# First block's mixer, front part: pooling as shifted sums with its counts in the weights, one rotation product per query head, gate half before value half, gate bias as one product

## The chip, the cores and the metric

The kernel runs on one core of one Trainium2 chip. The metric is the device time of one execution in microseconds (us), of which the median over runs counts. Engines are TensorE (PE, with PEld for its weight loads), VectorE (DVE), ScalarE (ACT), GpSimd (POOL) and SyncE (SP, which issues most DMAs).

## What is computed

The program is a chain of two transformer models over a sequence of 512 tokens of width 1024. The change touches only the mixer of the first model, which has two layers (`b0` and `b1`). Cut to what matters:

```python
p = h @ w_in[l]                       # 384 q, 256 kv, 32 k_rope, 256 pooling, 256 u, 256 v
# attention: latent queries and keys, 8 heads, 64 columns without and 32 with rotation
cq, ckv = rmsnorm(h_q, q_norm), rmsnorm(h_kv, kv_norm)
q_rope = [t1 * cos - t2 * sin, t1 * sin + t2 * cos]
s = q_nope . k_nope + q_rope . k_rope ; p = softmax(s * scale) ; out = p @ v
# pooling: groups of 64 columns, windows 2, 4, 8, 16 centred on t and clipped to the sequence
mean = (cs[hi] - cs[lo]) / (hi - lo)
out_g = (mean - h_g) @ w_pool[g] * pool_scale
# spatial gate: u and v, 4 heads of 64 columns, chunks of 128 tokens
z = gelu(h_uv) ; u, v = split(z) ; v = rmsnorm(v per head)
mixed = einsum('gpq,bcqgd->bcpgd', w_s, v) + b_s
out = u * mixed
```

After it come the output projection and the feed-forward of each layer, then the second model.

## The kernel before, in words

All activations are held with features on partitions and the 512 tokens along the free dimension. Every engine has its own program, written out by hand, and waits on semaphores (`wait_ge(..., at(engine, mark))`) for a mark that another engine sets when its instruction is done (`did(engine, mark)`). There is no scheduler: an engine works strictly in the order of its program, so whatever stands behind a waiting instruction waits too.

Large products take float32 numbers as a high and a low part (`hH`, `hL`; weights `WH`, `WL`) and add three products per 128 rows (`three`, L2621). Weights come in numbered chunks through two slots: SP loads `raw` (`load`, L503), ScalarE rounds it to `WH` (`hi`, L757), GpSimd subtracts to get `WL` (`low_parts`, L698), TensorE waits for that (`chunk`) and marks the slot as used. `c` is the first chunk of the layer's `w_in`; `c + 4` and `c + 5` hold u and v.

`first_mixing(l)` exists once for each engine. TensorE's goes: projections q, kv, k_rope and pooling (`p0`, `p1`) into the four banks `G`; sums of squares for the two norms; `spread_roots` (L2754), which spreads a norm's reciprocal roots over all partitions and waits for VectorE's reciprocal (L1494); u into `S[0]`, `S[1]`; v token by token chunk into `G[k]` (256 columns); the transposes of `w_s` (L2915); eight query heads through four banks `G[h % 4]`; the pooling products (L2941); 16 gate products (L2949), each followed by one that adds the bias (L2950, one partition row against `ones`); keys and values; then the attention loop, whose first instruction is the score product L2975.

VectorE's goes: rotation of the key (`rotate`, L1799 to L1802: two products and a sum); the norm of q (L1517 and L1509 in turn with ScalarE's rounding L814); clearing the padded rows `prow` and `pw` and copying `p0`, `p1` (L1629 to L1634); the norm of kv; for both halves of the pooling columns all four window sizes as shifted sums (L1649), each wanted half multiplied by the reciprocal counts `pool_inv` (L1656) and less the row itself (L1659); the statistics of v (L1666 to L1672); the rotation of each query head, three instructions with a 32 x 512 shape; the scaling of v (L1682, L1685); the pooled and gated outputs parted into high and low (L1527, L1529); eight copies of the rotated key (L1703); the attention loop.

The wait that ties them: a query head's product into a bank waits until VectorE has rotated the head that was in it.

```python
if h >= 4:
    pe.wait_ge(dve_done, at("dve", f"{n}.q{h - 4}.r"))
...
rotated_queries(0, 2)
V.tensor_tensor(v3, v3, vr[:, :].unsqueeze(2).broadcast_to([P, 16, 64]), ALU.mult)
```

## Time and profile before

| what | value |
|---|---|
| three runs, median | 3288.6 us (3285.46 to 3291.47) |
| the profiled execution, its own time | 3287.65 us |
| its span (first to last instruction) | 3285.8 us |
| mean granted TensorE clock over the span | 0.977 |
| TensorE busy | 3156.8 us, 96% |
| VectorE busy | 1878.1 us, 57% |
| front part of the mixer in layer 0, from the first u product to the first score product | 73.33 to 162.23 us |

The page gives shares of the whole span. The front part touched here is some 89 us long and comes twice, so it is read by stretches and in order of time. A granted clock of 1.0 is 2.4 GHz, 0.5 is 1.2 GHz. A float32 product that is not split into high and low parts shows as two records (xcount 2 for one instruction). The span is 1.85 us shorter than the execution's own time.

### The profile page before, as it was taken

Reading aid. Unit: us, or ns where it says so; the run is one execution under the profiler, and the core shown is the slowest. Engines: PE = TensorE matmul, PEld = TensorE weight load, DVE = VectorE, ACT = ScalarE, POOL = GpSimd, SP = SyncE. Lnnn points to the kernel's source line nnn. Section 1 sums busy time; section 2 is a strip of 40 time slices with the busy share of each in tenths; the row PEclk is TensorE's granted clock in tenths of the full one; section 3 lists DMA queues with packets and bytes.
Section 4 is the critical chain, followed back from the end, with each engine's and each line's share of the span. In section 5 each row is a group of like instructions: output and inputs, shape, how many; then the busy total and the mean of one; then the engine's idle time right before and its main releaser. Section 6 shows DMA issues by size and latency. Waiting matters only on the chain.

```text
span 3285.8 us, 42019 instructions
## 1 busy us (share of the span) xinstructions
PE 3156.8 (96%) x16648; PEld 2576.4 (78%) x16648; DVE 1878.1 (57%) x2970; ACT 1173.5 (36%) x1843; POOL 1245.3 (38%) x562
## 2 busy tenths in 40 slices
PE   8899999998999999999999999889999999999998
PEld 7647888876479888777888998758888687778887
DVE  4764777847544554674435877559665538453223
ACT  4353222232545433323336555332222325432222
POOL 4203444533037433334245454224444320134443
PEclk9899999998999999999999999899999999999999
DMA  7203545523035322223233333225554220113331
GB/s 131 61 13 95 157 142 174 181 66 71 13 95 165 99 87 81 77 71 96 90 110 104 111 111 112 98 70 179 160 178 137 77 73 14 39 58 97 97 96 64
DMA packets 480370, 324.40 MB, mean 99 GB/s; under 512 B 102336, under 2 KB 447552, under 8 KB 479664
## 3 DMA queue, kind: packets, MB, share of 16 engines
q1 hardware_dynamic: 475472, 310.10, 32.2%
q10 hardware_dynamic: 2656, 6.30, 0.5%
q0 software_dynamic: 2048, 5.32, 0.5%
q8 instruction: 132, 2.16, 0.3%
q14 instruction: 62, 0.51, 0.0%
HBM read 316.41 MB, written 5.24 MB: 98 GB/s over the span
## 4 chain that ended last, share of the span: by engine, by line
PE 85%; DVE 10%; ACT 3%; POOL 1%; issue 1%; DMA 0%; DVEq 0%; ACTq 0%; POOLq 0%
PE G L2630 11%; PE G L2631 11%; PE G L2635 11%; PE G L2621 11%; PE G L2846 6%; PE G L2847 5%; PE G L2851 5%; PE G L2646 2%; PE S L2975 2%; PE M L3052 2%; PE G L3693 1%; POOL WL L698 1%; PE S L2621 1%; ACT WH L757 1%; PE G L3042 1%
## 5 line engine op out<-in xcount | busy, mean ns | idle before, releaser
L698 POOL TENSOR_TENSOR WL<-raw,WH 128x1024 fp32r<-128x1024 f32 (+1 forms) x520 | 1224.6, 2377 | 1920.5 <-ACT WH L757 1920.5
L757 ACT ACTIVATE WH<-raw 128x1024 fp32r<-128x1024 f32 (+1 forms) x520 | 492.3, 995 | 607.4 <-PE G L2851 425.4
L2630 PE MATMUL G<-hH,WH 128*128 128x512 f32 x1520 | 594.8, 391 | 0.0
L2631 PE MATMUL G<-hL,WH 128*128 128x512 f32 x1520 | 591.9, 389 | 0.0
L2635 PE MATMUL G<-hH,WL 128*128 128x512 f32 x1520 | 360.1, 389 | 0.0
L2630 PEld LDWEIGHTS G<-hH,WH 128*128 128x128 f32 x1520 | 285.4, 188 | 60.7 <-ACT t_s L1198 0.8
L2635 PEld LDWEIGHTS G<-hH,WL 128*128 128x128 f32 x1520 | 285.3, 188 | 59.3
L2631 PEld LDWEIGHTS G<-hL,WH 128*128 128x128 f32 x1520 | 285.4, 188 | 58.7
L1550 DVE SCALAR_TENSOR_TENSOR acc<-adaw,cvec,acc 128x512 f32<-128x512 f32 x280 | 250.7, 948 | 4.2
L2621 PE MATMUL G<-hH,WH 128*128 128x512 f32 (+1 forms) x400 | 155.7, 389 | 14.8 <-POOL WL L698 14.8
L2621 PE MATMUL G<-hH,WL 128*128 128x512 f32 (+1 forms) x400 | 152.9, 382 | 0.0
L2621 PE MATMUL G<-hL,WH 128*128 128x512 f32 (+1 forms) x400 | 152.9, 382 | 0.0
L1574 DVE TENSOR_TENSOR FH<-silu,G 128x512 fp32r<-128x512 f32 x44 | 30.3, 688 | 212.7 <-PE G L2635 156.6
L2846 PE MATMUL G<-FH,WH 128*128 128x512 f32 x352 | 143.0, 406 | 0.2 <-DVE xT L1590 0.2
L2847 PE MATMUL G<-FL,WH 128*128 128x512 f32 x352 | 140.7, 400 | 0.0
L824 ACT ACTIVATE silu<-G 128x512 f32<-128x512 f32 x44 | 26.3, 599 | 271.5 <-PE G L2635 262.8
L1577 DVE TENSOR_TENSOR FL<-silu,FH 128x512 fp32r<-128x512 f32 x44 | 107.5, 2444 | 1.5
L1487 DVE TENSOR_TENSOR rstd<-rstd,sq 128x512 f32<-128x512 f32 (+1 forms) x84 | 61.5, 732 | 78.9 <-ACT sq L795 73.3
L1574 DVE TENSOR_TENSOR m_FH<-m_silu,G 128x512 fp32r<-128x512 f32 x22 | 15.1, 688 | 149.8 <-PE G L2635 147.5
L2621 PEld LDWEIGHTS G<-hH,WH 128*128 128x128 f32 x400 | 77.1, 193 | 30.0 <-POOL WL L698 15.7
L2621 PEld LDWEIGHTS G<-hL,WH 128*128 128x128 f32 x400 | 77.0, 192 | 14.5 <-issue 0.7
L2621 PEld LDWEIGHTS G<-hH,WL 128*128 128x128 f32 x400 | 76.9, 192 | 14.4
(699 smaller groups left out, 6402.7 us busy)
## 6 DMA issues: line engine op xcount, KB each, us to landing
raw<-ffn_w_in_in SPq DMA_DIRECT2D x264, 256.0 KB, 3.4
adaw<-ada_w_in SPq DMA_DIRECT2D x48, 1024.0 KB, 5.3
raw<-ab_w_in_in SPq DMA_DIRECT2D x128, 256.0 KB, 3.0
raw<-ffn_w_out_in SPq DMA_DIRECT2D x96, 256.0 KB, 2.9
raw<-w_gate_in SPq DMA_DIRECT2D x88, 256.0 KB, 3.3
raw<-w_up_in SPq DMA_DIRECT2D x88, 256.0 KB, 3.4
raw<-w_down_in SPq DMA_DIRECT2D x64, 256.0 KB, 2.9
raw<-w_in_in SPq DMA_DIRECT2D x40, 256.0 KB, 3.3
```

The costliest lines, as they stand in the source:

```text
L698: nc.gpsimd.tensor_tensor(WL[c % 2][:, cut], raw[c % 2][:, cut], WH[c % 2][:, cut].bitcast(F32), ALU.subtract)\
L757: nc.scalar.activation(WH[c % 2][:, cut], raw[c % 2][:, cut], ACT.Copy).then_inc(weights_hi, 1)
L1550: V.scalar_tensor_tensor(sums[:, b, i, :], weights[h % 2][:, k, :], col, sums[:, b, i, :], ALU.mult, ALU.add)\
L1577: V.tensor_tensor(FL[:, j, :], silu[:, t % 2, :], FH[:, j, :].bitcast(F32), ALU.subtract).then_inc(dve_done, did("dve", f"{n}.FL{t}"))
L2621: last = mm(dst, x, y, start=(k == 0 and j == 0), stop=(k == K - 1 and j == 2))
L2630: mm(dst, view(WH[c % 2], k), high, start=(k == 0 and not (joint and i)), stop=False)
L2631: mm(dst, view(WH[c % 2], k), low, start=False, stop=False)
L2635: last = mm(dst, view(WL[c % 2], k), X(k)[0], start=False, stop=(k == K - 1 and not (joint and i == 0)))
L2646: last = mm(dst, x, y, start=(k == 0 and j == 0 and not (joint and i)), stop=(k == K - 1 and j == 2 and not (joint and i == 0)))
L2846: mm(dst, part(WH, k, cols, o), high, start=(k == 0 and not (joint and i)), stop=False)
L2847: mm(dst, part(WH, k, cols, o), low, start=False, stop=False)
L2851: last = mm(dst, part(WL, k, cols, o), X(k)[0], start=False, stop=(k == count - 1 and not (joint and i == 0)))
```

## The change

- Pooling. ScalarE, no longer VectorE, copies `p0` and `p1` to `prow`. Only the window sizes that a half needs are summed; the last goes straight to `pd`. There is no product with counts: 1/w is multiplied into `w_p` once per layer, the first and last 8 tokens are corrected by `edges`, and the subtraction of the row is a second TensorE product with `w_n = -w_p`. Window work of half 0 stands before the q norm, of half 1 inside it.
- Order on TensorE. v (the gate half) comes in chunk `c + 4`, before u in `c + 5`; the spread of the kv norm stands between v1 and v2; then pooling products, transposes of `w_s`, u into `G[0]`, `G[1]`; query heads 0 to 3; the gate products; query heads 4 to 7; keys and values.
- Gate bias. One 33-row product of 512 columns per half opens the bank (L2982 of the changed kernel), in place of 16 products.
- Rotation. `qT` and `kT` use all 128 rows: 32 rows q times cos and 32 rows swapped q times sin, against the rotated key in both. The score product adds them, so a head takes one VectorE instruction.
- GpSimd's start gets four small clears and one DMA more; SP's table shrinks from 1024 to 34 columns.

The diff, cut to its core:

```diff
-    cols["pool_inv"] = inv.reshape(P, -1)
...
+        edge[r, g // 2] = np.stack([w / inside[:8], w / inside[T - 8:]])
+        share[r, g // 2] = 1.0 / w
+    cols["pool_edge"] = np.concatenate([share, edge.reshape(P, -1)], axis=1)
...
-                for n in range(3):
...
+                for n, block in enumerate((0, 2, 1)):
...
+                    load(c + 3 + n, columns(c + 3 + n, w, r0 + ROPE + block * 2 * P))
...
+                    nc.gpsimd.memset(b_s[:, :, :], 0.0).then_inc(pool_done, 1)
+                    nc.gpsimd.memset(bsel[:, :], 0.0).then_inc(pool_done, 1)
+                    pool.wait_ge(pool_done, 5)
+                    for g in range(2):
+                        nc.gpsimd.memset(bsel[32 * g:32 * g + 1, 64 * g:64 * g + 64], 1.0).then_inc(pool_done, 1)
...
+                    pool.dma_start(b_s[32 * g:32 * g + 1, :, :], a["b_s"][l:l + 1].rearrange("o (k g) p -> o g k p", g=2)[:, g]).then_inc(sides_loaded, 16)
...
-                stats(f"{n}.nq", 3, lambda k: latq[:, k, :], lat_fresh)
...
+                def pool_rows(k):
+                    act.wait_ge(pe_done, at("pe", f"{n}.p{k}"))
+                    nc.scalar.activation(prow[:, k, PAD:PAD + T], G[2 + k][:, :], ACT.Copy).then_inc(act_done, did("act", f"{n}.prow{k}"))
+
+                def gate_rows(k):
+                    act.wait_ge(pe_done, at("pe", f"{n}.v{k}"))
+                    nc.scalar.activation(vg[:, k, :], G[k][:, 0:SGW], ACT.Gelu_apprx_tanh).then_inc(act_done, did("act", f"{n}.vg{k}"))
+
+                for k in range(3):
+                    if k == 2:
+                        pool_rows(0)
+                    square(f"{n}.nq", k, latq[:, k, :], lat_fresh)
+                stats_before[0] = f"{n}.nq.sum"
+                root(f"{n}.nq", T // P, QL)
                 for k in range(2):
...
+                pool_rows(1)
...
+                gate_rows(0)
+                gate_rows(1)
...
+                gate_rows(2)
+                gate_rows(3)
+                hi(c + 6)
+                act.wait_ge(dve_done, at("dve", f"{n}.vrec"))
+                nc.scalar.activation(vr[:, :], vr[:, :], ACT.Sqrt).then_inc(act_done, did("act", f"{n}.vr"))
+                act.wait_ge(pe_done, at("pe", f"{n}.wsT"))
+                nc.scalar.activation(w_sT[:, :, :].rearrange("p g q -> p (g q)"), G[2][:, :], ACT.Copy).then_inc(act_done, did("act", f"{n}.wsT"))
...
+                    nc.scalar.activation(ug[:, k, :], G[k][:, :], ACT.Gelu_apprx_tanh).then_inc(act_done, did("act", f"{n}.ug{k}"))
...
+                V.tensor_scalar(w_n[:, :, :], w_p[:, :, :], -1.0, None, ALU.mult).then_inc(dve_done, did("dve", f"{n}.wn"))
...
+                    V.tensor_scalar(w_p[:, k, :], w_p[:, k, :], pool_edge[:, k:k + 1], None, ALU.mult).then_inc(dve_done, did("dve", f"{n}.wp"))
+                for o in (PAD - 8, PAD + T):
+                    V.memset(prow[:, :, o:o + 8], 0.0).then_inc(dve_done, did("dve", f"{n}.pz"))
...
-                rotate(n, "kr", G[1], krope[64:96, :])
...
-                V.memset(prow[:, :, :], 0.0).then_inc(dve_done, did("dve", f"{n}.pz"))
-                V.memset(pw[:, :, :], 0.0).then_inc(dve_done, did("dve", f"{n}.wz"))
...
-                    V.tensor_copy(prow[:, k, PAD:PAD + T], G[2 + k][:, :]).then_inc(dve_done, did("dve", f"{n}.prow{k}"))
...
+                V.tensor_copy(krope[96:128, :], krope[64:96, :]).then_inc(dve_done, did("dve", f"{n}.kr.2"))
...
+                def windows(k):
+
+                    dve.wait_ge(act_done, at("act", f"{n}.prow{k}"))
+                    src = prow[:, k, :]
+                    for w, (back, ahead) in enumerate(((1, 0), (1, -1), (2, -2), (4, -4))[:2 * k + 2]):
+                        dve.wait_ge(dve_done, here())
+                        if w % 2 and w // 2 == k:
+                            V.tensor_tensor(pd[64:128, k, :], src[64:128, PAD - back:PAD - back + T], src[64:128, PAD - ahead:PAD - ahead + T], ALU.add)\
+                                .then_inc(dve_done, did("dve", f"{n}.w{k}{w}"))
+                            continue
...
                         V.tensor_tensor(dst[:, o:o + m], src[:, o - back:o - back + m], src[:, o - ahead:o - ahead + m], ALU.add)\
                             .then_inc(dve_done, did("dve", f"{n}.w{k}{w}"))
...
-                            V.tensor_tensor(pd[r:r + 64, k, :], dst[r:r + 64, PAD:PAD + T], pool_inv[r:r + 64, k, :], ALU.mult)\
-                                .then_inc(dve_done, did("dve", f"{n}.pm{k}{w}"))
...
-                            V.tensor_tensor(pd[r:r + 64, k, :], pd[r:r + 64, k, :], prow[r:r + 64, k, PAD:PAD + T], ALU.subtract)\
...
+                            V.tensor_copy(pd[0:64, k, :], dst[0:64, PAD:PAD + T]).then_inc(dve_done, did("dve", f"{n}.pc{k}"))
+                    dve.wait_ge(dve_done, here())
+                    for e, o in enumerate((0, T - 8)):
+                        V.tensor_tensor(pd[:, k, o:o + 8], pd[:, k, o:o + 8], edges[:, k, e, :], ALU.mult).then_inc(dve_done, did("dve", f"{n}.pd{k}"))
+
+                windows(0)
+                mean(f"{n}.nq")
+                windows(1)
+                normed(f"{n}.nq", 3, lambda k: latq[:, k, :], lambda k: g_q[:, l, k:k + 1], cqH, cqL)
+                mean(f"{n}.nkv")
+                normed(f"{n}.nkv", 2, lambda k: latkv[:, k, :], lambda k: g_kv[:, l, k:k + 1], ckH, ckL)
...
+                def rotated_query(h):
+
+                    dve.wait_ge(pe_done, at("pe", f"{n}.qh{h}"))
+                    V.tensor_tensor(qT[64:128, h, :], G[(h + 3) % 4][64:128, :], trig[64:128, :], ALU.mult).then_inc(dve_done, did("dve", f"{n}.q{h}.r"))
...
-                        rotate(n, f"q{h}", G[h % 4], qT[64:96, h, :])
...
+                    V.tensor_scalar(hH[:, 4 + k, :], S[k][:, :], g_pool[:, l, k:k + 1], None, ALU.mult).then_inc(dve_done, did("dve", f"{n}.mH{4 + k}"))
...
+                    V.scalar_tensor_tensor(hL[:, 4 + k, :], S[k][:, :], g_pool[:, l, k:k + 1], hH[:, 4 + k, :].bitcast(F32), ALU.mult, ALU.subtract)\
...
+                for h in range(4):
+                    rotated_query(h)
+                    if h in (1, 2):
+                        pooled(h - 1)
+                for h in range(4, NH):
+                    rotated_query(h)
+                    if h % 2:
+                        k = h // 2 - 2
+                        dve.wait_ge(pe_done, at("pe", f"{n}.sg{k}"))
+                        dve.wait_ge(act_done, at("act", f"{n}.ug{k}"))
+                        dve.wait_ge(dve_done, here())
+                        V.tensor_tensor(ht[:, k, :], M[k][:, :], ug[:, k, :], ALU.mult).then_inc(dve_done, did("dve", f"{n}.sgo{k}"))
+                        parted(6 + k, n)
...
-                    V.tensor_copy(kT[64:96, h, :], krope[64:96, :]).then_inc(dve_done, did("dve", f"{n}.kr{h}"))
...
+                    V.tensor_copy(kT[64:128, h, :], krope[64:128, :]).then_inc(dve_done, did("dve", f"{n}.kr{h}"))
...
-                project(c + 4, 0, S[0], "u0")
-                project(c + 4, 1, S[1], "u1")
...
-                spread_roots(f"{n}.nkv")
...
+                        spread_roots(f"{n}.nkv")
+                        pe.wait_ge(act_done, at("act", f"{n}.prow1"))
...
+                    pe.wait_ge(dve_done, at("dve", f"{n}.pd{k}"))
+                    mm(S[k][:, :], w_p[:, k, :], pd[:, k, :], start=True, stop=False)
+                    mm(S[k][:, :], w_n[:, k, :], prow[:, k, PAD:PAD + T], start=False, stop=True).then_inc(pe_done, did("pe", f"{n}.pool{k}"))
+                pe.wait_ge(sides_loaded, 16 * SIDES * (l + 1))
+                pe.wait_ge(act_done, at("act", f"{n}.vg2"))
+                for g in range(4):
+                    last = nc.tensor.transpose(G[2][:, g * P:g * P + P], w_s[:, g, :], ident[:, :])
+                last.then_inc(pe_done, did("pe", f"{n}.wsT"))
+                chunk(c + 5)
+                project(c + 5, 0, G[0], "u0")
+                project(c + 5, 1, G[1], "u1")
                 tally.also("pe", f"used.{c + 5}")
...
+                        if h < 4:
+                            pe.wait_ge(act_done, at("act", f"{n}.{('vg3', 'ug0', 'ug1', 'wsT')[h]}"))
+                        else:
+                            pe.wait_ge(act_done, at("act", f"{n}.qn{h - 4}"))
+                            pe.wait_ge(dve_done, at("dve", f"{n}.q{h - 4}.r"))
...
+                queries(0, 4)
...
-                    mm(S[k][:, :], w_p[:, k, :], pd[:, k, :], start=True, stop=True).then_inc(pe_done, did("pe", f"{n}.pool{k}"))
...
+                    mm(M[k][:, :].rearrange("p (c t) -> p c t", c=4), bsel[:, :], b_s[:, k, :].unsqueeze(1).broadcast_to([33, 4, P]), start=True, stop=False)
...
-                            mm(dst, vg[:, c4, head * 64:head * 64 + 64], w_sT[:, head, :], start=True, stop=False)
-                            last = mm(dst, ones[0:1, 0:64], b_s[0:1, head * P:head * P + P], start=False, stop=True)
...
+                            last = mm(dst, vg[:, c4, head * 64:head * 64 + 64], w_sT[:, head, :], start=False, stop=(c4 == 3))
...
+                queries(4, NH)
...
-                        mm(S[s % 2][:, :], qT[0:QK, h, i * P:i * P + P], kT[0:QK, h, :], start=True, stop=True).then_inc(pe_done, did("pe", f"{n}.sc{s}"))
...
+                        if i == 0:
+                            pe.wait_ge(dve_done, at("dve", f"{n}.kr{h}"))
+                        mm(S[s % 2][:, :], qT[:, h, i * P:i * P + P], kT[:, h, :], start=True, stop=True).then_inc(pe_done, did("pe", f"{n}.sc{s}"))```

**VectorE, layer 0, behind the key's rotation.** `ncol` is the reciprocal of a norm, `ht` the normed row. Before:

```order
L1494 RECIPROCAL ncol<-M 128x4
L1517 SCALAR_TENSOR_TENSOR ht<-latq,g_q,M 128x512 x2
L1509 TENSOR_TENSOR cqL<-ht,cqH 128x512
L1517 SCALAR_TENSOR_TENSOR ht<-latq,g_q,M 128x512
L1509 TENSOR_TENSOR cqL<-ht,cqH 128x512 x2
L1629 MEMSET prow 128x1088
L1630 MEMSET pw 128x1088
L1634 COPY prow<-G 128x512 x2
L1494 RECIPROCAL ncol<-M 128x4
```

Of the change:

```order
L1522 RECIPROCAL ncol<-M 128x4
L1681 TENSOR_TENSOR pw<-prow 128x526
L1681 TENSOR_TENSOR pw<-pw 128x524
L1681 TENSOR_TENSOR pw<-pw 128x520
L1686 COPY pd<-pw 64x512
L1675 TENSOR_TENSOR pd<-pw 64x512
L1689 TENSOR_TENSOR pd<-pd,pool_edge 128x8 x2
L1545 SCALAR_TENSOR_TENSOR ht<-latq,g_q,M 128x512 x2
L1537 TENSOR_TENSOR cqL<-ht,cqH 128x512
L1545 SCALAR_TENSOR_TENSOR ht<-latq,g_q,M 128x512
L1537 TENSOR_TENSOR cqL<-ht,cqH 128x512 x2
L1522 RECIPROCAL ncol<-M 128x4
```

The clears and copies behind the q norm are gone, and the sums of half 1 now stand between the q norm's reciprocal and its first row. The second reciprocal still comes last.

**TensorE, layer 0, end of the v products.** `WH_54`, `WH_55` are the two weight slots. Before (the end of v1, the transposes, the start of v2):

```order
L2621 MATMUL G<-WL_57,hH 128x256
L2621 MATMUL G<-WH_55,hL 128x256
L2915 MATMUL S<-ident,w_s 128x128 x4
L2621 MATMUL G<-WH_55,hH 128x256
L2621 MATMUL G<-WL_57,hH 128x256
```

Of the change (the end of v3, then the start of u):

```order
L2654 MATMUL G<-WL_56,hH 128x256
L2654 MATMUL G<-WH_54,hL 128x256
L2947 MATMUL S<-pd,w_p 128x512
L2948 MATMUL S<-prow,w_n 128x512
L2947 MATMUL S<-pd,w_p 128x512
L2948 MATMUL S<-prow,w_n 128x512
L2952 MATMUL G<-ident,w_s 128x128 x4
L2654 MATMUL G<-hH,WH_55 128x512
L2654 MATMUL G<-hL,WH_55 128x512
```

The pooling products moved from behind the queries to here, doubled, and u follows v.

**TensorE, layer 0, the gate products.** Before, behind query head 7 (the last two rows come eight times for each half):

```order
L2621 MATMUL G<-cqL,WH_55 128x512
L2621 MATMUL G<-cqH,WL_57 128x512
L2941 MATMUL S<-pd,w_p 128x512 x2
L2949 MATMUL M<-w_sT,vg 64x128
L2950 MATMUL M<-b_s,ones 64x128
```

Of the change, between query heads 3 and 4:

```order
L2654 MATMUL G<-cqH,WL_56 128x512
L2982 MATMUL M<-b_s,bsel 128x512
L2987 MATMUL M<-w_sT,vg 64x128 x8
L2982 MATMUL M<-b_s,bsel 128x512
L2987 MATMUL M<-w_sT,vg 64x128 x8
L2654 MATMUL G<-cqH,WH_55 128x512
```

Sixteen bias products became two, and the stretch has query heads on both sides.

## Rows read from the trace of the kernel before

**Rows 1.** The page: busy time by engine; the chain that ended last.
```profile
PE 3156.8 (96%) x16648; PEld 2576.4 (78%) x16648; DVE 1878.1 (57%) x2970; ACT 1173.5 (36%) x1843; POOL 1245.3 (38%) x562
PE 85%; DVE 10%; ACT 3%; POOL 1%; issue 1%; DMA 0%; DVEq 0%; ACTq 0%; POOLq 0%
```

**Rows 2.** TensorE in order of time, block 0 (start us, us, engine, line ...).
```profile
73.33 0.48 PE L2621 MATMUL S<-hH,WH 128*128 128x512 f32 x1
...
84.31 1.05 PE L2754 MATMUL M<-ident,ncol 128*128 128x128 f32 x8
85.12 0.36 PE L2621 MATMUL G<-WH,hH 128*128 128x256 f32 x1
...
90.96 0.60 PE L2915 MATMUL S<-ident,w_s 128*128 128x128 f32 x4
...
97.87 0.47 PE L2621 MATMUL G<-cqH,WH 128*128 128x512 f32 x1 [0.56 <-ACT vg L887]
...
106.10 0.40 PE L2621 MATMUL G<-cqH,WL 128*128 128x512 f32 x1
112.49 0.76 PE L2621 MATMUL G<-cqH,WH 128*128 128x512 f32 x1 [6.00 <-DVE qT L1802]
...
122.43 0.79 PE L2621 MATMUL G<-cqH,WH 128*128 128x512 f32 x1 [2.94 <-DVE qT L1802]
...
129.40 1.88 PE L2941 MATMUL S<-pd,w_p 128*128 128x512 f32 x4
131.21 0.43 PE L2949 MATMUL M<-w_sT,vg 128*64 128x128 f32 x2
...
135.17 0.68 PE L2950 MATMUL M<-b_s,ones 1*64 1x128 f32 x2
...
148.12 0.80 PE L2621 MATMUL G<-ckH,WH 128*128 128x512 f32 x1
...
161.06 0.40 PE L2621 MATMUL G<-WH,ckL 128*128 128x512 f32 x1
162.23 1.95 PE L2975 MATMUL S<-kT,qT 96*128 96x512 f32 x4 [0.78 <-ACT vtok L911]
```

**Rows 3.** Busy time by stretch (PE, PEld, DVE, ACT, POOL; granted clock).
```profile
122.40:128.50 6.10, 6.07 (x15) 4.77 (x16) 5.62 (x9) 0.59 (x1) 0.00 (x0) 0.51 0.00 0
135.00:152.00 17.00, 17.00 (x53) 9.15 (x52) 9.62 (x17) 0.89 (x2) 1.31 (x1) 0.51 0.18 60
```

**Rows 4.** VectorE in order of time, block 0.
```profile
65.77 0.18 DVE L1494 RECIPROCAL ncol<-M 128x4 f32<-128x4 f32 x1 [6.36 <-ACT M L778]
73.62 1.53 DVE L1517 SCALAR_TENSOR_TENSOR ht<-latq,g_q,M 128x512 f32<-128x512 f32 x2 [7.66 <-PE M L2754]
...
76.45 1.48 DVE L1509 TENSOR_TENSOR cqL<-ht,cqH 128x512 fp32r<-128x512 f32 x2
...
81.76 0.18 DVE L1494 RECIPROCAL ncol<-M 128x4 f32<-128x4 f32 x1
...
92.47 2.77 DVE L1656 TENSOR_TENSOR pd<-pw,pool_inv 64x512 f32<-64x512 f32 x1
...
97.47 0.71 DVE L1649 TENSOR_TENSOR pw<-prow 128x526 f32<-128x526 f32 x1
...
106.42 1.22 DVE L1666 TENSOR_TENSOR vsq<-vg 128x1024 f32<-128x1024 f32 x1
...
109.14 0.25 DVE L1672 RECIPROCAL vr<-vr 128x16 f32<-128x16 f32 x1
...
150.14 2.77 DVE L1703 COPY kT<-krope 32x512 f32<-32x512 f32 x8
```

**Rows 5.** GpSimd in order of time, block 0.
```profile
16.90 10.75 POOL L698 TENSOR_TENSOR WL<-raw,WH 128x1024 fp32r<-128x1024 f32 x4 [6.25 <-ACT WH L757]
...
90.59 4.11 POOL L698 TENSOR_TENSOR WL<-raw,WH 128x512 fp32r<-128x512 f32 x2 [7.60 <-ACT WH L757]
```

**Rows 6.** TensorE in order of time, block 1.
```profile
834.67 1.52 PE L2975 MATMUL S<-kT,qT 96*128 96x512 f32 x3 [0.78 <-ACT vtok L911]
```

138 lines of the change are left out of this document (50 added, 88 removed).

## The prediction

> **What bounds the kernel now.** I first read the busy times and the chain on the page: TensorE is busy for 96% of the span and carries 85% of the chain, so the kernel as a whole is bound by TensorE [rows 1]. That average hides the stretch that the change touches. I therefore read TensorE in order of time, from the first u product (73.33) to the first score product (162.23), and sorted those 88.9 us into three kinds [rows 2]. First, dense products: 36 query products from 97.87 to 106.10 are 0.235 us apart; 48 u products take 10.98 us, 48 of v with half the columns 5.84 us. Second, idle time: 6.00 us before query head 4 and 2.94 us before a later head, both ended by VectorE's rotation; 0.56 us before head 0 and 0.78 us before the first score. Third, small products: sixteen gate and sixteen bias products, from 131.21 to 148.12.
>
> The stretches add the granted clock [rows 3]. It is 0.51 (the level of 1.2 GHz) from 122.4 to 128.5, behind the idle 2.94 us, and again from 135 to 152, although TensorE was busy for 17.00 of those 17.00 us. There a small product went from 0.36 us (131.21 to 135.17, eleven steps) to 0.62 us (135.17 to 148.12, 21 steps) [rows 2]. So the clock fell with nothing waiting, some 4 us into the small products.
>
> VectorE's order of time tells why TensorE waited [rows 4]. It ran the sums of pooling until the statistics of v began at 106.42, and only then came to the query heads, three instructions each. Its products of two SBUF operands take 0.71 us alone (97.47) and 2.77 us beside GpSimd (92.47), which subtracts from 90.59 on [rows 4, 5].
>
> Layer 1 repeats all this: its first score product comes at 834.67, 672.44 us after that of layer 0 [rows 2, 6]. So I cost one layer and take it twice.
>
> **The change, part by part: start of the piece.** GpSimd's extra clears and DMA come before its first subtraction at 16.90, which waited 6.25 us for ScalarE [rows 5]: nothing, and at most a few us once if that cover were gone. SP's smaller table comes earlier, not later: nothing. VectorE's small clears and scaled weights fall into its idle time before the key's rotation. The sums of pooling half 0 now stand before the q norm's reciprocal at 65.77, for which VectorE waited 6.36 us; two sums of 0.71, one copy of 0.35 (2.77 / 8) and two tiny products make 2.2 us with their gaps. Even all of it behind 65.77 would be over at 68.2, and TensorE asks for that reciprocal only just before 73.33 [rows 2, 4]. So the gate half starts at 73.33, as u did.
>
> **One new wait.** The spread of the kv norm now stands behind v1, and it needs a reciprocal that VectorE makes after the q norm. Before, VectorE worked from 73.62 to 77.93 on the q norm and then on clears and copies until the reciprocal at 81.76 [rows 4]. Now half 1's sums come first: four of 0.71, a copy and two tiny products, 3.6 us with gaps; the q norm ends at about 81.5 and the reciprocal at about 81.9, as before. But TensorE asks earlier: v0 and v1 end at 73.33 + 5.84 = 79.17. **TensorE is idle for 2.7 us** where it was not. Queued behind it are v2, v3 and all the rest.
>
> **TensorE's sum at 2.4 GHz**, from 73.33: v0 and v1 5.84; idle 2.7; spread 0.81 (84.31 to 85.12); v2 and v3 5.84; four float32 products of 512 columns at 0.905 (two took 129.40 to 131.21), 3.6, of which 1.8 are new; transposes 0.36; u 10.98; queries 0 to 3 (36 x 0.235) 8.5; gate products 2 x (0.905 for the bias + 8 x 0.36) = 7.6, where sixteen pairs would be 11.5; queries 4 to 7 8.5; 48 key and value products at 0.235, 11.3; and 0.94 from the last of them to the first score (161.29 to 162.23) [rows 2]. Together 67.0, so the first score product comes at 140.3. That is **21.9 us earlier** in each layer.
>
> The bias product has 33 rows and 512 columns, which no row shows; I take the 0.905 of a full one, between the 0.36 of a small one and twice 0.905, since time followed columns and not rows above: a one-row bias product took the same 0.36 as a 128-row one. Score products go from 96 to 128 rows: nothing, by the same comparison.
>
> **What must keep up.** The statistics of v start when v3 is out (88.6) and take 3.0 us as before (106.42 to 109.39); with a square root and two scalings, even at 2.77 us each, they are done before 100, and the gate products want them at 112 [rows 4]. The rotation is one product a head, at most 0.71 us, against nine products or 2.1 us of TensorE; each head that came late all the same would cost up to 0.71. The keys' copies (2.77) and the parted outputs follow query head 7, which is out at 128, with 12 us until the first score. If a weight chunk were late, TensorE would idle for GpSimd's 4.11 us a chunk [rows 5]; the chunk for queries 4 to 7 gets its slot when u is through (103.7), so it is ready near 110 and wanted at 120.
>
> **The clock.** Two places lie in new circumstances. Behind the new idle 2.7 us: a gap of 2.94 us was followed by 6.97 us (122.43 to 129.40) for 18 products that take 4.2 us at 2.4 GHz, a loss of 2.8. Bounds are 0 and 2.8; I take 2.8, the nearest row. In the small products: the clock fell 4.0 us in and came back at about 152.1, 4.0 us after they ended. Of 7.6 us, 4.0 pass at full speed, 3.6 become 3.6 x 0.62 / 0.36 = 6.2 (+2.6), and the next 4.0 us of dense products, at some 1.8 times their length, lose 1.8: 4.4 together. Bounds: 0, and 7 if it fell at once.
>
> The Trainium skill says otherwise of the second place. "TensorE: Matmul & The Clock Gate", section "What's actually happening": the throttled clock is the default state and activity releases it. By that rule a stretch without a gap keeps its clock, and the 4.4 us would be nothing. This trace does not agree: the row of 135 to 152 has full busy time and clock 0.51.
>
> **Sum.** 21.9 - 2.8 - 4.4 = 14.7 us a layer, 29.4 us in all. Against the profiled execution's own 3287.65 us (span 3285.8 and 1.85 around it) that is 3258.3; the median of the three runs is 0.95 higher, so 3259.2 us.
>
> **The rivals.**
>
> *The clock holds in the small products.* The bias products, one row of 128, were half of the old stretch, and in their place stand long ones; that speaks for it, the row at 135 against. It gives back 2 x 4.4 = 8.8: 3250.4. If it also holds behind the gap, 5.6 more: 3244.8. The rule above is this rival's ground; as far as the trace bears it out, chance 0.28 for both together.
>
> *VectorE meets GpSimd.* The q norm comes 3.6 us later, and with it the rounding and subtraction of u's chunk, close to the kv reciprocal. If one or two of VectorE's products stretch from 0.71 to 2.77 before it, the idle time at v2 grows by 2.1 to 4.2 us, and later waits at the gate products could follow. Two such products a layer: 2 x 4.2 = 8.4 back, 3267.6. For it: 92.47. Against: GpSimd's subtraction follows ScalarE's rounding, which follows VectorE's own last q row. Chance 0.20.
>
> *The clock does not come back.* After the idle time at v2 come pooling products, transposes and gate products, none of them dense, and the clock could stay at 1.2 GHz through u and the queries too. From 82.7 to 139 lie 57 us of products. Behind the gap at 122.43 the work took 1.66 times as long and twice is the most at half the clock; at 1.8 they would grow by 46 us, against 21.9 saved: 24 slower a layer, 3337. It decides from 27 us of full-speed work at 1.2 GHz on. Against: dense products brought the clock back within 7 us behind each gap. Chance 0.03.
>
> **Numbers.** Forecast 0.46, clock holding 0.28, contention 0.20, clock lost 0.03, a small loss or gain from something else 0.03. What a measurement of this kernel tells from no change is about 0.2%, 6.6 us. Faster by more: 0.94; within: 0.03; slower by more: 0.03. Range: from the case in which the clock holds everywhere (3244.8, less 1.8 for the runs' own spread) to the contention case with one or two stretched products more, 3271.
>
> **What would show it.** In the changed profile: first score product near 147.5 instead of 162.23, and 74 us instead of 89 behind 73.33; idle time of 2.7 us before the kv norm's spread, ended by the reciprocal; no idle time before query heads 4 to 7; a granted clock near 0.5 at the gate products; six pooling sums a layer on VectorE instead of eight, and no 64 x 512 product behind them. The forecast is wrong if TensorE waits at the queries for ScalarE, or for weights behind u, or if the attention loop itself gets slower with 128 rows.

## The result, and the profile after

The changed kernel takes **3241.1 us** (median of four runs, 3240.71 to 3241.75) against 3287.0 us of the kernel before (four runs, 3285.10 to 3291.47): a ratio of 0.9859, 95% interval 0.9842 to 0.9876. The gain is 46 us where 29.4 were forecast. The time lies 18.1 us below the forecast of 3259.2, 1.9 us below the range and 3.7 us below the rival in which the clock holds everywhere. Run again later beside other kernels it took 3242.1 us (e12), 0.9854 of the kernel before.

The profiled execution took 3241.41 us, for a span of 3239.4. From the page of the changed kernel, the busy time by engine and the chain that ended last:

```profile
PE 3124.9 (96%) x16600; PEld 2562.3 (79%) x16600; DVE 1834.0 (57%) x2930; ACT 1179.3 (36%) x1849; POOL 1245.4 (38%) x568
...
PE 87%; DVE 8%; ACT 2%; POOL 1%; issue 1%; DMA 1%; SPq 0%; ACTq 0%; DVEq 0%
```

TensorE is still busy for 96% of the span and carries the chain; its busy time fell by 31.9 us [rows 1]. So two thirds of the gain is work that TensorE no longer does or does faster, and not waiting that went away. The page can't say which work. TensorE in order of time does, in layer 0 of the changed kernel (columns as in [rows 2]):

```profile
74.20 0.36 PE L2654 MATMUL G<-WH,hH 128*128 128x256 f32 x1
...
82.81 1.16 PE L2787 MATMUL M<-ident,ncol 128*128 128x128 f32 x8 [2.61 <-DVE ncol L1522]
83.72 0.36 PE L2654 MATMUL G<-WH,hH 128*128 128x256 f32 x1
...
89.55 1.02 PE L2947 MATMUL S<-pd,w_p 128*128 128x512 f32 x2
...
92.98 0.60 PE L2952 MATMUL G<-ident,w_s 128*128 128x128 f32 x4
...
104.35 0.40 PE L2654 MATMUL G<-cqH,WH 128*128 128x512 f32 x1
...
112.85 1.12 PE L2982 MATMUL M<-b_s,bsel 33*128 33x512 f32 x2
113.90 1.09 PE L2987 MATMUL M<-w_sT,vg 128*64 128x128 f32 x16
114.92 1.12 PE L2982 MATMUL M<-b_s,bsel 33*128 33x512 f32 x2
115.98 1.09 PE L2987 MATMUL M<-w_sT,vg 128*64 128x128 f32 x16
...
117.00 0.50 PE L2654 MATMUL G<-cqH,WH 128*128 128x512 f32 x1
...
137.60 1.96 PE L3017 MATMUL S<-kT,qT 128*128 128x512 f32 x4 [0.73 <-issue]
```

The gate half starts at 74.20 (forecast 73.33), waits once for 2.61 us (forecast 2.7) and never at a query head. Then comes the place that decides: the two bias products and sixteen gate products run from 112.85 to 117.00. That is **4.15 us** where the kernel before took 16.9 for the same results (131.21 to 148.12) [rows 2], and where 7.6 were forecast. Eight gate products take 1.02 us (113.90 to 114.92), 0.13 each. The first score product comes at 137.60, not at 162.23: 24.6 us earlier. Layer 1, in the same view:

```profile
722.19 0.36 PE L2654 MATMUL G<-WH,hH 128*128 128x256 f32 x1
...
730.79 2.08 PE L2787 MATMUL M<-ident,ncol 128*128 128x128 f32 x8 [2.61 <-DVE ncol L1522]
...
787.03 1.53 PE L3017 MATMUL S<-kT,qT 128*128 128x512 f32 x3 [0.73 <-issue]
```

There it comes at 787.03, not at 834.67 [rows 6]: 47.6 us earlier over both layers. The spans differ by 46.4, so 1.2 us were given back in the rest of the program. That is within what executions of one kernel differ by there: behind the first score of layer 1 the changed kernel takes 2452.4 us here and 2448.9 us in e12. The granted clock in the changed kernel, by stretch (columns as in [rows 3]):

```profile
81.00:89.50 8.50, 6.69 (x56) 6.69 (x57) 5.56 (x8) 5.89 (x9) 4.74 (x2) 1.00 0.29 55
112.80:117.00 4.20, 4.20 (x37) 2.29 (x36) 1.21 (x2) 2.49 (x3) 2.43 (x2) 1.00 0.30 105
117.00:130.00 13.00, 13.00 (x58) 10.51 (x57) 7.99 (x10) 6.00 (x10) 4.97 (x3) 1.00 0.24 83
729.30:735.00 5.70, 4.21 (x23) 4.21 (x24) 3.30 (x6) 5.43 (x8) 4.25 (x2) 0.70 0.13 32
```

In the front part the clock holds at its upper level behind the new wait of layer 0, through the small products of both layers (1.00 from 762.28 to 766.43 too) and behind them; only behind the wait of layer 1 is it down for a part (0.70).

So the 25.5 us of layer 0 (88.9 before, 63.4 now, from the first product of the u or the v half, whichever comes first, to the first score) come from: small products 16.9 to 4.15, 12.8 us; idle time on TensorE 10.3 to 3.3, 6.9 us; the slow clock behind the old waits of 6.00 and 2.94 us, 5.6 (18 products each in 7.0 us that take 4.2 at full clock); the slow clock in the first key and value products, 1.9 (48 products in 13.2 us, not 11.3); and 1.7 us the other way, for two more pooling products.

### The profile page after: what moved, and what is told of

Same layout as the page of the kernel before. It is cut to its first block, busy times and chain, and to the rows that moved or that the text cites. A ratio compares the mean times of both kernels' runs of the same rounds, so it can differ in the third digit from the quotient of the medians.

```text
span 3239.4 us, 41902 instructions
## 1 busy us (share of the span) xinstructions
PE 3124.9 (96%) x16600; PEld 2562.3 (79%) x16600; DVE 1834.0 (57%) x2930; ACT 1179.3 (36%) x1849; POOL 1245.4 (38%) x568
## 4 chain that ended last, share of the span: by engine, by line
PE 87%; DVE 8%; ACT 2%; POOL 1%; issue 1%; DMA 1%; SPq 0%; ACTq 0%; DVEq 0%
PE G L2654 13%; PE G L2663 12%; PE G L2664 12%; PE G L2668 11%; PE G L2879 6%; PE G L2880 6%; PE G L2884 6%; PE G L2679 2%; PE S L3017 2%; PE M L3094 2%; PE G L3735 1%; POOL WL L713 1%; ACT WH L772 1%; PE G L3084 1%; PE S L3759 1%
## 5 line engine op out<-in xcount | busy, mean ns | idle before, releaser
L2663 PEld LDWEIGHTS G<-hH,WH 128*128 128x128 f32 x1520 | 285.4, 188 | 60.6 <-ACT t_s L1226 0.8
L2668 PEld LDWEIGHTS G<-hH,WL 128*128 128x128 f32 x1520 | 285.4, 188 | 59.2
L2664 PEld LDWEIGHTS G<-hL,WH 128*128 128x128 f32 x1520 | 285.4, 188 | 58.6
L2654 PE MATMUL G<-hH,WH 128*128 128x512 f32 (+1 forms) x432 | 170.0, 393 | 14.8 <-POOL WL L713 14.8
L2654 PE MATMUL G<-hH,WL 128*128 128x512 f32 (+1 forms) x432 | 167.3, 387 | 0.0
L2654 PE MATMUL G<-hL,WH 128*128 128x512 f32 (+1 forms) x432 | 167.0, 386 | 0.0
L2654 PEld LDWEIGHTS G<-hH,WH 128*128 128x128 f32 x432 | 84.5, 196 | 31.5 <-POOL WL L713 15.7
L2654 PEld LDWEIGHTS G<-hL,WH 128*128 128x128 f32 x432 | 84.2, 195 | 15.9 <-issue 0.7
L2654 PEld LDWEIGHTS G<-hH,WL 128*128 128x128 f32 x432 | 84.0, 194 | 16.0
```

What stands on the lines that cost most here:

```text
L2654: last = mm(dst, x, y, start=(k == 0 and j == 0), stop=(k == K - 1 and j == 2))
L2663: mm(dst, view(WH[c % 2], k), high, start=(k == 0 and not (joint and i)), stop=False)
L2664: mm(dst, view(WH[c % 2], k), low, start=False, stop=False)
L2668: last = mm(dst, view(WL[c % 2], k), X(k)[0], start=False, stop=(k == K - 1 and not (joint and i == 0)))
```

## The experiments

All times are medians of four runs, with the ratio to the kernel before, run beside them. The changed kernel is at 3241 to 3242 us.

| run | kernel | us | ratio, 95% interval |
|---|---|---|---|
| e1 | changed, a one-row bias product behind each gate product | 3270.1 | 0.9942 (0.9925 to 0.9959) |
| e2 | changed, eight one-row bias products first | 3243.5 | 0.9862 (0.9847 to 0.9876) |
| e3 | changed, one-row bias and gate in turn, never the same place | 3260.2 | 0.9918 (0.9903 to 0.9933) |
| e4 | changed, kv reciprocal ahead of the sums of half 1 | 3234.2 | 0.9838 (0.9824 to 0.9853) |
| e5 | before, with the bias as one product | 3259.2 | 0.9907 (0.9892 to 0.9921) |
| e6 | before, with the one-product rotation | 3269.0 | 0.9938 (0.9923 to 0.9953) |
| e7 | changed, with the old rotation | 3249.3 | 0.9878 (0.9862 to 0.9895) |
| e8 | e4, and one pooling product a half | 3236.5 | 0.9836 (0.9821 to 0.9851) |
| e9 | changed, a 33-row bias product behind each gate product | 3263.7 | 0.9916 (0.9901 to 0.9931) |
| e10 | before, with e5's and e6's edits | 3247.3 | 0.9870 (0.9856 to 0.9885) |
| e11 | e4 again | 3234.7 | 0.9834 (0.9819 to 0.9849) |
| e12 | the changed kernel again | 3242.1 | 0.9854 (0.9838 to 0.9871) |
| e13 | changed, a 128-row bias product behind each gate product | 3240.3 | 0.9850 (0.9834 to 0.9867) |
| e14 | changed, gate products by head | 3245.8 | 0.9869 (0.9854 to 0.9884) |

### Why a gate product takes 0.13 us and not 0.36

**e1** puts sixteen pairs back into the changed kernel:

```diff
-mm(M[k][:, :].rearrange("p (c t) -> p c t", c=4), bsel[:, :], b_s[:, k, :].unsqueeze(1).broadcast_to([33, 4, P]), start=True, stop=False)
...
-last = mm(dst, vg[:, c4, head * 64:head * 64 + 64], w_sT[:, head, :], start=False, stop=(c4 == 3))
+places = [(c4, g) for c4 in range(4) for g in range(2)]
+dst = lambda c4, g: M[k][64 * g:64 * g + 64, c4 * P:c4 * P + P]
+bias = lambda c4, g, **kw: mm(dst(c4, g), ones[32 * g:32 * g + 1, 0:64], b_s[32 * g:32 * g + 1, k, :], **kw)
+gate = lambda c4, g, **kw: mm(dst(c4, g), vg[:, c4, (2 * k + g) * 64:(2 * k + g) * 64 + 64], w_sT[:, 2 * k + g, :], **kw)
+for c4, g in places:
+    gate(c4, g, start=True, stop=False)
+    last = bias(c4, g, start=False, stop=True)
```

> The changed kernel with the old bias form: behind each of the 16 gate products a one-row bias product into the same place. Theory A (the alternation itself makes each of the 32 products 0.36 us instead of 0.13, and the thin stretch lets the clock fall): the gate stretch of a layer grows from 4.15 us to 11.5 us at the full clock and to 15 to 17 us with the clock falling as before, so 3241.1 plus 15 to 29 us, 3256 to 3270 us. Theory B (the slow products of before came from a clock that had already fallen twice at the waits for the rotation): no fall here, since the queries around are dense; 11.5 us a layer and 3256 us. Rival C (16 short products more cost only their own 0.13 us): 3241 us or a little below.

Measured 3270.1 us: this one edit gives back 29 of the 46 us. TensorE in order of time, layer 0 of e1, and below it the clock of a stretch inside:

```profile
111.88 0.43 PE L2985 MATMUL M<-w_sT,vg 128*64 128x128 f32 x2
112.24 0.43 PE L2984 MATMUL M<-b_s,ones 1*64 1x128 f32 x2
112.60 0.43 PE L2985 MATMUL M<-w_sT,vg 128*64 128x128 f32 x2
...
149.84 1.53 PE L3018 MATMUL S<-kT,qT 128*128 128x512 f32 x3 [0.73 <-issue]
```

```profile
119.20:127.00 7.80, 7.80 (x27) 3.72 (x26) 0.00 (x0) 0.00 (x0) 0.00 (x0) 0.50 0.22 69
```

Each product starts 0.36 us behind the one before, and from 118 on, at half the clock, 0.62. The stretch takes 15.4 us (111.88 to 127.23) with TensorE busy throughout. So a gate product of the same shape costs 0.36 us here and 0.13 in the changed kernel: its price is no property of the product alone, but comes with the products around it.

**e2** issues the same sixteen one-row products, but eight ahead of the eight gate products:

```diff
...
+for c4, g in places:
+    bias(c4, g, start=(c4 == 0), stop=False)
+for c4, g in places:
+    last = gate(c4, g, start=False, stop=(c4 == 3))
```

> The same 16 one-row bias products, but all 8 of a half ahead of its 8 gate products, so that neither the row count alternates nor two products in a row go to the same place. Theory A (alternation costs): 8 x 0.13 us for the biases of a half in place of 1.05 us, so the time of the changed kernel, 3241 us within 1. Rival (one-row products are slow by themselves, 0.36 us each): 16 x 0.36 = 5.8 in place of 2.1 us a layer, 3248.5 us.

```profile
112.84 1.09 PE L2984 MATMUL M<-b_s,ones 1*64 1x128 f32 x16
113.86 1.09 PE L2985 MATMUL M<-w_sT,vg 128*64 128x128 f32 x16
114.88 1.09 PE L2984 MATMUL M<-b_s,ones 1*64 1x128 f32 x16
115.90 1.89 PE L2985 MATMUL M<-w_sT,vg 128*64 128x128 f32 x16
...
139.09 1.96 PE L3019 MATMUL S<-kT,qT 128*128 128x512 f32 x4 [0.73 <-issue]
```

In these rows of layer 0 of e2 eight one-row products take 1.02 us too. With 3243.5 us it stands within 2.4 us of the changed kernel. So the number of products was not the cost, and the one long bias product is worth hardly more than the same work grouped. The fourth row is longer because the clock fell in it, 3.2 us behind the start of the stretch (0.54 from 115.90 to 117.72, TensorE busy throughout), in this layer only; in layer 1 the same stretch takes 4.09 us at the full clock.

**e3** asks whether the second product of a pair waits for the first in the same place. Here the bias of the next place stands ahead of each gate product, so neighbours never write the same place:

```diff
...
+bias(*places[0], start=True, stop=False)
+for j in range(8):
+    if j < 7:
+        bias(*places[j + 1], start=True, stop=False)
+    last = gate(*places[j], start=False, stop=True)
```

> One-row bias and 128-row gate products alternate, but each bias product goes to the place of the next gate product, so no two in a row write the same place. If the cost is the switch between 1 and 128 rows: as e1. If it is that a product waits for the one before it in the same place: as e2, 3241 us.

Measured 3260.2 us. The products are still 0.36 us apart (112.13, 112.50, 112.85, 113.22 in its trace) and the clock falls again; the first score comes at 146.83. The place is not the cause. e3 is 10 us better than e1, with a shorter time at half the clock (stretch 12.9 us, not 15.4); why was not followed. In e9 below the same stretch takes 15.0 us in one layer and 12.95 in the other, so the length of the slow part is not fixed within one kernel either.

**e9** replaces the one row by 33 rows, the selector's 64 columns of that head:

```diff
-mm(M[k][:, :].rearrange("p (c t) -> p c t", c=4), bsel[:, :], b_s[:, k, :].unsqueeze(1).broadcast_to([33, 4, P]), start=True, stop=False)
...
-last = mm(dst, vg[:, c4, head * 64:head * 64 + 64], w_sT[:, head, :], start=False, stop=(c4 == 3))
+mm(dst, vg[:, c4, head * 64:head * 64 + 64], w_sT[:, head, :], start=True, stop=False)
+last = mm(dst, bsel[:, 64 * g:64 * g + 64], b_s[:, k, :], start=False, stop=True)
```

> The changed kernel with the bias again behind each gate product (sixteen and sixteen in turn, as in e1), but each bias product now has 33 rows (the selector's 64 columns for that head) and not one. Theory 1, what is dear is the change to and from a product of ONE row: here a product takes some 0.13 us, the stretch of 32 products some 4.2 us, the clock holds, and the time is that of the changed kernel, 3241 to 3244 us. Theory 2, every change between unlike numbers of rows costs the 0.23 us that the trace of e1 shows: a product takes 0.36 us, the granted clock falls in the stretch, 3270 us as e1. Between them (3250 to 3260): a price that grows as the rows become fewer.

Theory 1, a price of the one row, is refuted. Measured 3263.7 us; again 0.36 us a product, and behind 119 the clock is down (order of time, then the stretches):

```profile
112.54 0.43 PE L2986 MATMUL M<-w_sT,vg 128*64 128x128 f32 x2
112.91 0.43 PE L2987 MATMUL M<-b_s,bsel 33*64 33x128 f32 x2
113.26 0.43 PE L2986 MATMUL M<-w_sT,vg 128*64 128x128 f32 x2
```

```profile
112.60:119.00 6.40, 6.40 (x37) 3.35 (x36) 1.10 (x2) 2.48 (x3) 4.64 (x2) 1.00 0.39 128
119.20:127.50 8.30, 8.30 (x28) 3.75 (x27) 0.00 (x0) 0.00 (x0) 0.00 (x0) 0.50 0.24 73
```

**e13** is e9 with 128 rows, all zero but two. Order, places and columns stay:

```diff
...
-("bsel", [33, P], F32), ("b_s", [33, 2, P], F32)
+("bsel", [P, P], F32), ("b_s", [P, 2, P], F32)
```

> As e9, but the bias products have 128 rows, all but two of them zero, so that every product of the stretch has the same number of rows; order, places and columns are those of e9. Theory 1, what is dear is that neighbours have unlike numbers of rows: here a product takes 0.13 us, or up to the 0.23 us that its 128 columns take at the pace of a product of 512 (0.905 us), the stretch of 32 products 4.2 to 7.2 us, the granted clock holds, and the time is 3241 to 3250 us. Theory 2, what is dear is that neighbours alternate between two products (gate, bias) that add into the same place, whatever their rows: 0.36 us each, the stretch 15 us and the clock down, as e9: 3264 us.

```profile
111.77 0.45 PE L2986 MATMUL M<-w_sT,vg 128*64 128x128 f32 x4
112.03 0.40 PE L2987 MATMUL M<-b_s,bsel 128*64 128x128 f32 x4
112.25 0.44 PE L2986 MATMUL M<-w_sT,vg 128*64 128x128 f32 x4
...
115.09 0.44 PE L2987 MATMUL M<-b_s,bsel 128*64 128x128 f32 x4
...
136.07 1.96 PE L3017 MATMUL S<-kT,qT 128*128 128x512 f32 x4 [0.73 <-issue]
```

```profile
111.80:115.40 3.60, 3.60 (x65) 3.49 (x64) 1.12 (x2) 2.49 (x3) 1.91 (x1) 1.00 0.31 105
```

Measured 3240.3 us. The same 32 products in the same turn take 3.69 us (111.77 to 115.46), 0.12 each, a third of 0.36, at a clock of 1.00. Between e9 and e13 only the number of rows differs. **The price is that of neighbours with unlike numbers of rows, 1 or 33 against 128.** It stands between the starts of the products and not in their length: a record of a gate product lasts 272 to 273 ns in both where the clock is up.

This fits a rule of the Trainium skill, in "TensorEngine Tiling (Array Packing)", section "Key Properties": changing the tiling mode, not only the tile, drains TensorE. The modes that this page of the Trainium skill lists have tiles of 128, 64 or 32 rows. The trace agrees as far as it goes: 0.36 against 0.12 us; the drain itself no row shows.

Not every unlike number costs. Scores of 96 rows stand between transposes of 128, and the 64 score records of a layer span 74.0 to 76.9 us from first to last with 96 rows (the kernel before, e5, e7) and 74.2 to 76.7 us with 128 (e4, e6, e10, the changed kernel). At the full clock the transpose starts 429 ns behind the last score record in both. The same page of the Trainium skill has no mode between 64 and 128 rows, which fits this too.

What the clock does with such a stretch these runs don't separate. It fell 4.0 us into the stretch of the kernel before, and 5.2 to 9.6 us into those of e6, e1, e3 and e9, with TensorE busy; e13's is over in 3.7 us and the changed kernel's in 4.15. So e13 shows the price of the turns, and not that equal rows keep the clock up. e2 lost the clock in one layer without such turns.

**e14** looks at the other half of the price, why eight products of 128 columns take 1.02 us, where eight quarters of a product of 512 columns (0.905) are 1.81. It sorts the gate products by head, so that neighbours write the same 64 partitions:

```diff
...
-for c4 in range(4):
-    for g in range(2):
+for g in range(2):
+    for c4 in range(4):
```

> The changed kernel with the eight gate products of a half in the order head, then token tile, so that four neighbours write the same 64 partitions; in the changed kernel neighbours write the lower and the upper 64 in turn. Theory A, neighbours on unlike halves run beside each other, which is why eight of them take 1.02 us where eight times a quarter of 0.905 is 1.81 us: here a half takes 1.8 us, 1.6 us more a layer, and the time is 3244 to 3246 us. Theory B, a product of 128 columns takes 0.13 us wherever it writes: the stretch keeps its 4.15 us and the time is 3241 to 3242 us.

```profile
114.66 1.12 PE L2982 MATMUL M<-b_s,bsel 33*128 33x512 f32 x2
115.71 1.58 PE L2987 MATMUL M<-w_sT,vg 128*64 128x128 f32 x16
117.22 1.12 PE L2982 MATMUL M<-b_s,bsel 33*128 33x512 f32 x2
118.27 1.58 PE L2987 MATMUL M<-w_sT,vg 128*64 128x128 f32 x16
```

Eight of them now take 1.51 us (118.27 to 119.78), half as much again as 1.02. So neighbours on unlike halves of the output partitions overlap in part. Whether it is the products or their weight loads that run beside each other, the rows don't tell. And 1.51 is still below 1.81, so the columns alone don't price even these; why was not followed. The same section of the Trainium skill says that tiles work independently; the trace agrees, 1.02 against 1.51 us. The new order costs 1 us a layer (stretch 5.13 us, not 4.15). The time (3245.8 us, runs from 3242.1 to 3248.6) went the expected way, but by more than 2 us, and these four runs don't settle the rest.

### What each part of the change is worth

**e5** (the kernel before, with the bias product alone) and **e6** (the kernel before, with the rotation alone):

```diff
 # e5
+mm(M[k][:, :].rearrange("p (c t) -> p c t", c=4), bsel[:, :], b_s[:, k, :].unsqueeze(1).broadcast_to([33, 4, P]), start=True, stop=False)
...
-mm(dst, vg[:, c4, head * 64:head * 64 + 64], w_sT[:, head, :], start=True, stop=False)
-last = mm(dst, ones[0:1, 0:64], b_s[0:1, head * P:head * P + P], start=False, stop=True)
+last = mm(dst, vg[:, c4, head * 64:head * 64 + 64], w_sT[:, head, :], start=False, stop=(c4 == 3))
...
 # e6
+V.tensor_copy(krope[96:128, :], krope[64:96, :]).then_inc(dve_done, did("dve", f"{n}.kr.2"))
...
-rotate(n, f"q{h}", G[h % 4], qT[64:96, h, :])
+V.tensor_tensor(qT[64:128, h, :], G[h % 4][64:128, :], trig[64:128, :], ALU.mult)
...
-mm(S[s % 2][:, :], qT[0:QK, h, ...], kT[0:QK, h, :], start=True, stop=True)
+mm(S[s % 2][:, :], qT[:, h, ...], kT[:, h, :], start=True, stop=True)
```

> The kernel before with one thing of the change: one 33-row bias product per half instead of 8 one-row products. Theory (e1 and e3: the alternation is the larger part of the gain): the gate stretch goes from 16.9 us to about 4.2 us and the 4 us of slow products behind it lose 1.8 us less, 14.6 us a layer, so 3288 - 29 = 3259 us. Rival (the clock still falls there, since queries with waits stand before it): 3265 to 3269 us.

> The kernel before with the rotation as one VectorE product per head and 128-row scores, nothing else. Theory (the waits at the queries are the smaller part): the wait of 6.00 us shrinks by 1.4 us, the second one of 2.94 us nearly goes, and with it 2.8 us of slow clock: 6 to 7 us a layer, 3274 to 3277 us. Rival (the query waits carry most of the gain): 3260 us or below. Score products of 128 rows instead of 96 cost nothing; if they did, the attention loop would be longer.

e5 came as expected: 3259.2 us. The bias product alone, with the clears and loads that it needs, brings 31.0 us, where the whole change brings 46 to 48. Its trace has the small products from 131.34 to 135.49, the same 4.15 us, with all the old waits ahead of them (6.00 us, and 4.04 where 2.94 was); the first score is at 147.98. e6 gained more than expected, 21.2 us. In its trace the wait before head 4 is still there (4.57 us, not 6.00), but the second one, of 2.94 us, is gone, and with it the slow clock behind it. From the first u product to the first score it takes 79.2 us in each layer, not 88.9:

```profile
110.62 0.72 PE L2623 MATMUL G<-cqH,WH 128*128 128x512 f32 x1 [4.57 <-DVE qT L1680]
...
152.09 1.95 PE L2977 MATMUL S<-kT,qT 128*128 128x512 f32 x4 [0.78 <-ACT vtok L911]
```

**e10** has both edits in the old order:

> The kernel before with both e5's bias product and e6's rotation, in the old order of the work and with the old pooling. Theory 1, the new order and the pooling in the weights are worth nothing of their own: from e6's first score (152.1 us) a stretch of small products of 4.15 us in place of 16.0 us and full clock behind it take 13.7 us, so the first score comes at 138.4 us, and the time is 3238 to 3243 us, as the changed kernel. Theory 2, the order carries a part: the old wait of 4.57 us before query head 4, with a slow clock behind it now that the small products no longer follow, puts the first score at 141 us or later, 3247 to 3252 us.

3247.3 us: 42.8 us, where the changed kernel beside it (e12) gained 48.0. So the parts overlap (31.0 + 21.2 = 52.2), and the new order with its pooling brings the last 5.2 us; the two were not taken apart. Its trace says how: from the first u product (73.04) to the first score (139.10) it takes 66.1 us, against 63.4 in e12. It waits 4.56 us before head 4 at a half clock behind it, against 2.61 us, and 0.56 us before head 0; two pooling products fewer give 1.7 us back. The intervals of the two ratios overlap, but the runs themselves do not (3246.6 to 3248.6, 3236.4 to 3242.3), and over both layers the front part is 4.6 us longer in e10's trace. From layer 0 of e10:

```profile
110.77 0.61 PE L2629 MATMUL G<-cqH,WH 128*128 128x512 f32 x1 [4.56 <-DVE qT L1686]
```

**e7** takes the rotation out of the changed kernel (three VectorE instructions a head, 96-row scores):

```diff
-V.tensor_tensor(qT[64:128, h, :], G[(h + 3) % 4][64:128, :], trig[64:128, :], ALU.mult)
+bank = G[(h + 3) % 4]
...
+V.tensor_tensor(qT[64:96, h, :], bank[64:96, :], trig[64:96, :], ALU.mult)
+V.tensor_tensor(ht[64:96, 0, :], bank[96:128, :], trig[96:128, :], ALU.mult)
+V.tensor_tensor(qT[64:96, h, :], qT[64:96, h, :], ht[64:96, 0, :], ALU.add)
...
-mm(S[s % 2][:, :], qT[:, h, ...], kT[:, h, :], start=True, stop=True)
+mm(S[s % 2][:, :], qT[0:QK, h, ...], kT[0:QK, h, :], start=True, stop=True)
```

> The changed kernel with the old rotation, three VectorE instructions per head and 96-row scores. Theory: 2.1 us of VectorE per head fit beside 2.1 us of TensorE now that pooling and the gate are done before; 0 to 1 us a layer, 3241 to 3243 us. Rival (the one-product rotation is what removed the waits): the waits of 2 to 6 us a layer come back, 3246 us or more.

3249.3 us, 8 more than the changed kernel; I had expected the new order to hide the old rotation. It doesn't. TensorE in order of time, layer 0 of e7, waits twice at the key and value products, and so in layer 1:

```profile
132.72 0.47 PE L2659 MATMUL G<-ckH,WH 128*128 128x512 f32 x1 [2.22 <-DVE qT L1724]
...
135.51 0.47 PE L2659 MATMUL G<-ckH,WH 128*128 128x512 f32 x1 [1.16 <-DVE qT L1724]
```

Two times 3.4 us is 6.8 of the 8; the rest is no more than what runs of one kernel differ by. In the changed kernel VectorE stands idle for 1.40 us between two heads with no other work between them (107.35 to 108.75 us).

### The one wait that the new order makes

**e4** lets VectorE take the kv norm's reciprocal before the pooling sums of half 1, so that the spread finds its operand ready:

```diff
 windows(0)
 mean(f"{n}.nq")
+normed(f"{n}.nq", 3, ...)
+roots(f"{n}.nkv")
 windows(1)
-normed(f"{n}.nq", 3, ...)
-mean(f"{n}.nkv")
+dve.wait_ge(pe_done, at("pe", f"{n}.nkv.bc"))
 normed(f"{n}.nkv", 2, ...)
```

> VectorE makes the kv norm's reciprocal before the pooling sums of half 1 instead of behind them; everything else as in the changed kernel. Theory: the 2.61 us that TensorE idles before the spread of the kv norm go in each layer, and the slow stretch behind it in layer 1 (1.4 us) with them: 3241.1 - 5.2 - 1.4 = 3234.5 us. Rival: the pooling sums then run beside GpSimd, end late, and TensorE idles before the pooling products instead: 3239 to 3242 us.

> e4's kernel once more, with more rounds, beside the changed kernel in the same job. If the wait of 2.61 us before the kv norm's spread and the slow clock that can follow it are worth two times 2.6 us and up to 2.8 us more, it is 5 to 8 us faster than the changed kernel (3233 to 3236 us against 3241 us). Rival: the first comparison was a matter of the chip, and the two are within 2 us.

> The changed kernel, beside e10 and e11 in the same job: 3241 us, 0.986 of the kernel before. If e10 equals it, order and pooling bring nothing; if e11 is 5 to 8 us below it, the one wait that the new order makes is what it gives away.

3234.2 us (e4) and 3234.7 us (e11). e12 ran beside e11 and took 3242.1, 7 us more; their runs overlap (3233.5 to 3239.2, 3236.4 to 3242.3), but taken with e4's and those of the first measurement, all eight runs of this version (3232.9 to 3239.6) lie below seven of the changed kernel's eight (3240.7 to 3242.3, the eighth at 3236.4). The traces show it directly. The products that spread the roots now start at 78.87, with nothing waited for, and from the first v product to the first score it takes 60.53 us in both layers of both e4 and e11, against 63.40 and 64.84 in the changed kernel. That is 7.2 us: two waits of 2.61 are 5.2, the slow clock behind the one of layer 1 is 1.4, and 0.3 a layer was not followed. The sums of half 1 now run beside GpSimd and stretch (2.45 us the first, from 78.43, not 0.71), but TensorE waits for none of them. This version is faster than both kernels.

```profile
78.87 1.05 PE L2788 MATMUL M<-ident,ncol 128*128 128x128 f32 x8
...
133.56 1.52 PE L3018 MATMUL S<-kT,qT 128*128 128x512 f32 x3 [0.73 <-issue]
```

The changed kernel's list of waits on TensorE has this row (us in total, times, longest), and e4's has none for it:

```profile
PE M L2787 <- DVE ncol L1522: 5.2, 2, 2.6
```

**e8** goes on from there and drops the two added pooling products, with the row subtracted on VectorE as before:

```diff
-V.tensor_scalar(w_n[:, :, :], w_p[:, :, :], -1.0, None, ALU.mult)
...
+V.scalar_tensor_tensor(pd[:, k, :], pd[:, k, :], pool_edge[:, k:k + 1], prow[:, k, PAD:PAD + T], ALU.mult, ALU.subtract)
...
-mm(S[k][:, :], w_p[:, k, :], pd[:, k, :], start=True, stop=False)
-mm(S[k][:, :], w_n[:, k, :], prow[:, k, PAD:PAD + T], start=False, stop=True)
+mm(S[k][:, :], w_p[:, k, :], pd[:, k, :], start=True, stop=True)
```

> e4 (the kv norm's reciprocal before the pooling sums of half 1), and the row subtracted by one VectorE instruction per half again, so that pooling is one TensorE product per half and not two: 1.7 us of TensorE less in each layer for 2 x 0.7 us of VectorE. Theory: 3234.2 - 3.4 = 3231 us. Rival (VectorE then ends the sums too late and TensorE waits for them): 3234 us or more.

3236.5 us, no gain over e4. The 1.7 us of TensorE are saved and waited away at once, in layer 0 (and by the same waits in layer 1):

```profile
87.03 1.12 PE L2947 MATMUL S<-pd,w_p 128*128 128x512 f32 x2 [0.19 <-DVE pd L1687]
...
89.69 0.63 PE L2951 MATMUL G<-ident,w_s 128*128 128x128 f32 x4 [1.53 <-ACT vg L890]
```

In the changed kernel the added pooling products cover ScalarE's gelu of the gate half; without them TensorE waits 1.53 us for that, and 0.19 us for VectorE's pooling rows.

## Why the prediction was wrong, step by step

The direction and the mechanism held: TensorE's path to the first score is what the change shortens, and it shortens it in both layers. The size was off: 3259.2 us forecast, 3241.1 measured. In the spans 17.0 us more were saved than forecast. The small products are 15.7 of that (two times 3.45 and 4.4), the clock behind the new wait 4.2, and some 3 us went the other way (later starts of both layers, 1.2 us in the rest of the program).

- **Start of the gate half: right.** 73.33 forecast, 74.20 measured, and in e12 73.25.
- **The new wait: right.** 2.7 us forecast, 2.61 measured, ended by the reciprocal as said. e4 confirms its place and price.
- **v, pooling products, transposes, u, queries, key and value products: right.** They were to take 55.9 us; 63.4 less 2.61, 4.15 and 0.91 for the spread leaves 55.7.
- **"Gate products 2 x (0.905 for the bias + 8 x 0.36) = 7.6": the step that failed.** Measured 4.15. The 0.36 was read in a stretch of products with 128 rows and 1 row in turn [rows 2], and carried over to a stretch in which the turns are gone. e1, e2, e9 and e13 show that 0.36 comes with the turn, and that without it a gate product takes 0.13. The rows held a warning that I read the other way. That a one-row product took the same 0.36 as a 128-row one, while a product of 512 columns took 0.905, I took as "time followed columns". But by columns 128 of them would be 0.226, and 0.36 is above that: something else was being paid. Columns would not have given the price either: 0.13 is below 0.226, in part because neighbours on unlike halves overlap (0.19 where they mostly don't, in e14). The bias product itself was well priced (1.05 with its changes of rows, 0.905 forecast).
- **"In the small products: ... 4.4 together": failed with it.** The clock held in both layers. By the prediction's own row, a fall 4.0 us into the stretch, a stretch of 4.15 us would have lost next to nothing; the loss was costed for one of 7.6. In all eight kept traces with the stretch of 4.15 us (the changed kernel, e12, and e4, e5, e7, e8, e10, e11) it held in both layers, and in e2 it fell 3.2 us into one of two stretches of that length. So the short stretch is enough to explain it, and by e2 that it held in both layers may be luck in part. Whether the turns also bring the clock down stays open.
- **"Behind the new idle 2.7 us: ... I take 2.8": half right.** Nothing in layer 0, and some 1.4 us in layer 1 (63.4 against 64.84 us from start to first score). Between 0 and 2.8, as bounded; the upper end was taken.
- **The sum.** Layer 0: forecast 14.7, plus 3.45 for the gate products, 4.4 and 2.8 for the clock, 0.1 for the rest, less 0.9 for the later start, is 24.55; measured 24.6.
- **The rotation: right, and unpriced.** It was costed at nothing since TensorE covers it; true of the new rotation. e7 shows that the old one would have cost 8 us in the new order, so it is no idle part of the change.
- **The rival "VectorE meets GpSimd": did not happen.** In layer 0 the first three sums of half 1 take 0.71 and 0.72 us each between 74.48 and 76.67, and the wait is 2.61. In e4, where the sums come later, they do meet it, and TensorE still does not wait.
- **The range** ended at the case in which the clock holds everywhere but small products still cost 0.36 us. No end of it was taken from a cheaper product, though no row of before showed gate products standing alone. The miss was on that side.

The rule weighed in the prediction, of "TensorE: Matmul & The Clock Gate", section "What's actually happening" in the Trainium skill, was judged by the row of 135 to 152: busy throughout, clock 0.51. e9's row of 119.20 to 127.50 repeats it (8.30 of 8.30 busy, 0.50), while the query products behind the small ones in the changed kernel, from 117.00 to 130.00, are busy 13.00 of 13.00 at 1.00. So the recorded busy time alone doesn't tell whether the clock holds. What else in the stretch does, no run here shows: e13, which took the turns away, is over sooner than the clock fell in any stretch with turns.

## What to carry to other kernels

The price of an instruction is that of its neighbours too: before a duration is carried from one stretch to another, ask whether it would be the same if the other instructions were not between, and let the range take in a cheaper price where no row shows the instruction without them. On TensorE, don't let products of few rows (a bias added by one row, a selector) take turns with full ones: group them, make one long product of them, or fill them with zero rows. The three ran within 3.2 us of each other here, and the turns cost 18 to 29 us more than the changed kernel. When a new order is made to feed TensorE, look for the one operand that now comes last; its reciprocal moved by a few lines was worth 7 us more.
